# Two-block layer stack on one core: odd stage in another order, first tail weights split ahead of the norms, small products of the even stage in pairs

## The chip, the core and the metric

One core of a Trainium2 chip runs the whole program. Its engines run side by side and meet only at semaphores: TensorE (PE, matrix products into eight PSUM banks), VectorE (DVE), ScalarE (ACT), GpSimd (POOL), and SyncE (SP), which issues nearly all loads. The metric is the device time in microseconds (us) of one execution.

## The reference

Tokens x (256 x 1024) pass a first block of two layers (windowed attention with experts, a bidirectional recurrence with experts; each expert layer reads 16 experts' gate, up and down matrices), and then a second block of two layers, "even" and "odd". All is float32. The change touches the second block and the hand-over to it:

```python
def modulate(x, shift, scale): return layer_norm_2(x) * (1 + scale) + shift
# even: gated linear attention (4 heads, 64 x 128 states, chunks of 64 tokens, both directions d)
att = where(tri, (q*exp(b-b_mid)) @ (k*exp(b_mid-b)).T, 0);  o = att @ v
ds  = (k*exp(b_end-b)).T @ v;   s[c+1] = exp(b_end)*s[c] + ds[c];   o += (q*exp(b)) @ s[c]
y_gla = rms_norm(o) * silu(gg)
# even: latent attention (8 heads of 64+32, 512 keys): y_mla = softmax(q k.T * scale) @ v * silu(mg)
y = concat(y_gla, y_mla) @ w_out;   x = layer_norm_2(ALPHA*x + gate*y, g, b)
# odd: f, f_gate, u, v, s_gate = split(h @ w_in)
y_f = real(fft2(f)) * silu(f_gate)                      # as products with cosine and sine tables
y_s = gelu(u) * (sgu_w @ layer_norm(gelu(v)) + sgu_b) * silu(s_gate)
x = layer_norm_2(ALPHA*x + gate * (concat(y_f, y_s) @ w_out), g, b)
```

## The kernel before

The token axis is two halves of 128 rows, the 1024 features are 8 tiles of 128. The program is written out engine by engine: every engine has its own instruction stream in a fixed order, and `Signals` turns named events into semaphore waits. So a wait at the head of an engine's stream holds everything behind it.

**Weights.** SP loads 2 MB units into a ring of seven slots in a fixed order (`loads`, `units`); a unit's load is issued when the former unit of its slot is "free". A tail unit is split into a rounded part (ACT, L348, four pieces) and the remainder (DVE, L364, four pieces), and each product with it is three passes of TensorE in the rounded format (L324 to L326). Other products are plain float32; the trace shows each of these as two instructions, here called passes.

**Norm and modulation.** After the last expert, DVE adds, takes moments, and norms x half by half (L451, L455, with the root on POOL, L461). `modulated_vector` then takes moments of both halves again (L1726), the root on POOL (L1767), writes `flat` (L1735); TensorE turns `flat` (L1717) between two runs of idle products with the identity (L369); DVE and ACT scale and shift (L1741, L1755), ACT rounds (L1760), DVE takes the remainder (L1746). Only then are the first weights of the stage split (`even_narrow`, `odd_f`).

**Even stage.** After the projections two generators are merged step by step, one step of `linear_*` and one of `latent_*` in turn, on every engine (`even_order`). The linear one: masked scores (L1963, 64 rows of the array a product), turning `kend` (L1973), att times values (L1986), then eight steps, each a read of a direction's state (L1996, 64 output columns of the array) and its state product (L2007), DVE updating the state (L2097), then copies out, squares (L1146), a norm (L1156, L2113), turning (L2022) and `yT` (L2121). States are kept as blocks of a 128 x 256 tile with zeros around them (memsets L2062 to L2064). The latent one: heads' queries and keys (L2220, L2223, one head a step, always output rows 0 to 63), values (L2229), and then 16 score rounds n (L2238, maximum L2324, exp L2378, scaling L2320, turning L2245, copy L2386), with the values product of a head in every second round (L2259, 64 output rows). PSUM banks 4 to 6 take scores and turned scores in turn. When both generators have ended come the output products: half 0 tile by tile (L412, two column blocks), then half 1 column block by column block (L425). `gated_residual_vector` works on a half as its blocks come in (L1780, L1782, L439), then norms it.

**Odd stage.** Five projection units in the order f, sv, su, fg, sg, two jobs each; then the turning of `sgu` (L2439), four rounds of the table products (L2449) and (L2456) with a copy `fc` between (L2501, L2552), the gate products (L2464), and the output products (L412, L425).

## Time and profile before

| | us |
|---|---|
| median of 3 runs | 1600.28 (1597.62 to 1602.88) |
| the profiled execution, device time | 1604.02 |
| its span, first to last instruction | 1602.5 |

Stages in the profiled execution, in us from the span's start: experts of both layers and the first block until about 1254.5, then the tail: hand-over and modulation to 1280.64, projections of the even stage to 1348.78, its two attentions to 1440.9, its output products to 1468.6, norm and modulation to 1488.2, projections of the odd stage to 1547.2, its mixing to 1566.7, its output products to 1594.2, last norm and store to the end. Rows of groups give busy time (overlaps within the group counted once), the mean ns of one instruction, and the idle time before them with what ended it.

### The profile page before, as it was taken

Reading aid. Unit: us, or ns where it says so; the run is one execution under the profiler, and the core shown is the slowest. Engines: PE = TensorE matmul, PEld = TensorE weight load, DVE = VectorE, ACT = ScalarE, POOL = GpSimd, SP = SyncE. Lnnn points to the kernel's source line nnn. Section 1 sums busy time; section 2 is a strip of 40 time slices with the busy share of each in tenths; the row PEclk is TensorE's granted clock in tenths of the full one; section 3 lists DMA queues with packets and bytes.
Section 4 is the critical chain, followed back from the end, with each engine's and each line's share of the span. In section 5 each row is a group of like instructions: output and inputs, shape, how many; then the busy total and the mean of one; then the engine's idle time right before and its main releaser. Section 6 shows DMA issues by size and latency. Waiting matters only on the chain.

```text
span 1602.5 us, 18908 instructions
## 1 busy us (share of the span) xinstructions
PE 1176.6 (73%) x8305; PEld 648.3 (40%) x8305; DVE 460.7 (29%) x940; ACT 299.6 (19%) x594; POOL 62.8 (4%) x88
## 2 busy tenths in 40 slices
PE   7998656687475556988775655656665799989987
PEld 6646211253131113984521111111111597545883
DVE  5535102101111003746420100100100567544524
ACT  4511010000310001291110000000000254340520
POOL 2000100000000000021000000000000100001000
PEclk9998788899778778999897787877867899999999
DMA  9909999999999999445999999999999622107310
GB/s 296 347 0 355 421 425 425 425 416 418 426 426 425 427 426 384 132 152 194 410 424 424 425 427 424 426 427 424 427 425 424 237 86 106 53 14 262 123 53 26
DMA packets 89761, 503.32 MB, mean 314 GB/s; under 512 B 7010, under 2 KB 15664, under 8 KB 56912
## 3 DMA queue, kind: packets, MB, share of 16 engines
q1 hardware_dynamic: 84320, 492.78, 75.9%
q10 hardware_dynamic: 3680, 8.04, 1.4%
q8 instruction: 65, 1.06, 0.3%
q0 software_dynamic: 1680, 1.30, 0.3%
q14 instruction: 16, 0.13, 0.0%
HBM read 501.00 MB, written 1.10 MB: 313 GB/s over the span
## 4 chain that ended last, share of the span: by engine, by line
DMA 50%; PE 33%; DVE 9%; ACT 5%; issue 1%; POOL 1%; SPq 1%; ACTq 0%; DVEq 0%
DMA weight_ring<-in_moe_w_gate_up 29%; DMA weight_ring<-in_moe_w_down 15%; PE bank L1285 5%; PE bank L324 3%; PE bank L325 3%; PE bank L326 3%; PE bank L1312 3%; PE bank L412 3%; DMA weight_spare<-in_ada_w 3%; PE bank L425 3%; DMA weight_ring<-in_even_w_in 2%; DVE weight_ring_rounded L364 1%; PE bank L2259 1%; PE bank L859 1%; DMA weight_ring<-in_lru_w_in 1%
## 5 line engine op out<-in xcount | busy, mean ns | idle before, releaser
L1285 PE MATMUL bank<-weight_ring,expert_tokens 128*32 128x512 f32 x2048 | 321.2, 763 | 205.0 <-DMA weight_ring<-in_moe_w_gate_up 199.0
L1285 PEld LDWEIGHTS bank<-weight_ring,expert_tokens 128*32 128x32 f32 x2048 | 66.6, 125 | 432.2 <-DMA weight_ring<-in_moe_w_gate_up 252.5
L1312 PE MATMUL bank<-weight_ring,actT 128*32 128x256 f32 x2048 | 170.8, 493 | 78.7 <-DMA weight_ring<-in_moe_w_down 68.8
L1312 PEld LDWEIGHTS bank<-weight_ring,actT 128*32 128x32 f32 x2048 | 77.9, 136 | 159.7 <-DMA weight_ring<-in_moe_w_down 68.7
L1406 DVE TENSOR_TENSOR act<-silu,bank 128x256 f32<-128x256 f32 x32 | 13.5, 421 | 435.1 <-ACT silu L1456 435.1
L1411 DVE COPY expert_outs<-bank 32x256 f32<-32x256 f32 x64 | 26.7, 418 | 272.2 <-PE bank L1312 271.2
L1456 ACT ACTIVATE silu<-bank 128x256 f32<-128x256 f32 x32 | 12.3, 384 | 482.0 <-PE bank L1285 481.9
L364 DVE TENSOR_TENSOR weight_ring_rounded<-weight_ring,weight_ring_rounded 128x1024 fp32r<-128x1024 f32 (+1 forms) x64 | 73.4, 1211 | 27.8 <-ACT weight_ring_rounded L348 27.7
L348 ACT CAST weight_ring_rounded<-weight_ring 128x1024 fp32r<-128x1024 f32 (+1 forms) x68 | 65.7, 1044 | 18.2 <-DMA weight_ring<-in_lru_w_in 11.6
L1465 ACT COPY expert_outs<-bank 32x256 f32<-32x256 f32 x64 | 23.3, 365 | 239.4 <-PE bank L1312 238.6
L461 POOL TENSOR_TENSOR norm_rstd<-norm_var,minus_half 128x1 f32<-128x1 f32 x12 | 18.3, 1527 | 932.5 <-DVE norm_var L449 932.5
L1296 PE MATMUL bank<-ident,act 128*128 128x128 f32 x64 | 17.7, 363 | 43.1 <-DVE act L1406 43.1
L1296 PEld LDWEIGHTS bank<-ident,act 128*128 128x128 f32 x64 | 10.1, 206 | 80.5 <-DVE act L1406 80.5
L369 PEld LDWEIGHTS bank<-ident 128*128 128x128 f32 x328 | 38.7, 197 | 1.4 <-issue 1.4
L324 PE MATMUL bank<-lru_x_hi_rounded,weight_ring_rounded 128*128 128x256 f32 x128 | 37.1, 289 | 2.8 <-DVE weight_ring_rounded L1575 1.8
L324 PE MATMUL bank<-odd_h_hi_rounded,weight_ring_rounded 128*128 128x256 f32 x128 | 37.1, 290 | 2.2 <-DVE weight_ring_rounded L364 2.2
L369 PE MATMUL bank<-ident 128*128 128x128 f32 x328 | 38.8, 280 | 0.0
L1329 PE MATMUL bank<-expert_outs,back 128*128 128x512 f32 x64 | 31.7, 622 | 9.3 <-DVE expert_outs L1411 7.9
L325 PE MATMUL bank<-odd_h_rounded,weight_ring_rounded 128*128 128x256 f32 x128 | 36.9, 288 | 0.0
L326 PE MATMUL bank<-odd_h_hi_rounded,weight_ring_rounded 128*128 128x256 f32 x128 | 36.8, 288 | 0.0
L325 PE MATMUL bank<-lru_x_lo_rounded,weight_ring_rounded 128*128 128x256 f32 x128 | 36.6, 286 | 0.0
L326 PE MATMUL bank<-lru_x_hi_rounded,weight_ring_rounded 128*128 128x256 f32 x128 | 36.5, 285 | 0.0
(460 smaller groups left out, 1803.3 us busy)
## 6 DMA issues: line engine op xcount, KB each, us to landing
weight_ring<-in_moe_w_gate_up SPq DMA_DIRECT2D x128, 2048.0 KB, 31.0
weight_ring<-in_moe_w_down SPq DMA_DIRECT2D x64, 2048.0 KB, 31.1
weight_ring<-in_ada_w SPq DMA_DIRECT2D x8, 2048.0 KB, 17.2
weight_ring<-in_even_w_in SPq DMA_DIRECT2D x5, 2048.0 KB, 14.6
weight_ring<-in_odd_w_in SPq DMA_DIRECT2D x5, 2048.0 KB, 8.1
weight_spare<-in_ada_w SPq DMA_DIRECT2D x4, 2048.0 KB, 20.7
weight_ring<-in_lru_w_in SPq DMA_DIRECT2D x4, 2048.0 KB, 23.5
weight_ring<-in_attn_w_qkv SPq DMA_DIRECT2D x2, 2048.0 KB, 15.5
```

Source lines behind the costliest of these rows:

```text
L324: self.pe.matmul(out, sl, mh, start=start, stop=False)
L325: self.pe.matmul(out, sh, ml, start=False, stop=False)
L326: return self.pe.matmul(out, sh, mh, start=False, stop=stop)
L348: a.copy(hi[:, c], raw[:, c]).then_inc(*sig.tell("weights_rounded", ("rounded", name, i)))
L364: v.tensor_tensor(lo[:, c], raw[:, c], hi[:, c], ALU.subtract).then_inc(*sig.tell("weights_split", ("weights", name, i)))
L369: self.pe.matmul(bank[:, 0:P], self.B.ident, self.B.ident, start=True, stop=True)
L412: last = pe.matmul(banks[2 * half + c], y[:, j, rows], w[c][:, j], start=(j == 0), stop=(j == T - 1))
L425: last = pe.matmul(banks[2 + c], y[:, j, P:2 * P], w[c][:, j], start=(j == 0), stop=(j == T - 1))
L1285: last = pe.matmul(up[CAP * j:CAP * (j + 1), :], B.xs[:, t, e * CAP:(e + 1) * CAP], w[:, t % 2, :, j, :], start=(t == 0), stop=(t == T - 1))
L1296: last = pe.transpose(K[2][:, s * P:(s + 1) * P], B.act[i][:, s::2], B.ident)
L1312: last = pe.matmul(K[3][CAP * q:CAP * (q + 1), 0:QC], B.actT[i][:, s, j * CAP:(j + 1) * CAP], w[:, jj, s, q, :], start=(j == 0 and s == 0) ...
L1329: pe.matmul(K[(4, 0)[c]], B.back[:, grp, half * P:(half + 1) * P], B.outs[grp % 2][:, c * 512:(c + 1) * 512], start=True, stop=True).then_ ...
```

## The change

In `experts_pool`, `modulated_vector`, `even_scalar` and `odd_scalar`: ACT rounds the stage's first two units before anything else of the stage, then works out `flat` of half 0 (new `flat_scalar`, six small and large activations with a root on POOL in between); DVE keeps half 1. POOL (new `split_weights_pool`) takes pieces 2 and 3 of `even_narrow`, DVE pieces 0 and 1, between `flat` and the modulation. In the odd stage DVE splits all of `odd_f` inside `gated_residual_vector` of the even stage, after half 0.

Even stage: products that use half of the array's rows or columns are issued in turn for the two halves: masked scores of both k, queries and keys of heads 2j and 2j+1 (the second to rows 64 to 127), values of two heads in every fourth round (with four `pT_lat` buffers). States are compact 128 x 128, without zeros. State products are 64 x 64 blocks of 128 columns over both directions; those of steps 0 and 1 come together, reads (split by row half kk) follow one or two at a time. Squares of `gla` are two activations and one DVE reduction, its scaling one instruction. The output products of tiles 0 to 3 (both halves) are eight more steps of the linear generator, and tiles 4 to 7 follow for half 0 and half 1.

Odd stage: projections f, sv, su; then the first table products and the turning of `sgu`; then fg; then the second table products and the gate products; then sg; then the output products. Banks and DVE's and ACT's orders follow.

```diff
+    def split_weights_pool(self, name, n, pieces):
...
+        for i in pieces:
+            c = slice(i * n // 4, (i + 1) * n // 4)
+            g.wait_ge(*sig.after("rounded", name, i))
+            g.tensor_tensor(lo[:, c], raw[:, c], hi[:, c], ALU.subtract).then_inc(*sig.tell("weights_split_here", ("weights", name, i)))
...
+        stage = f"moe{layer}"
+        self.norm_pool(stage, 0)
+        if layer == 0:
+            self.norm_pool(stage, 1)
+            return
+        narrow = T * sum(n for _, n in EVEN_W[0][1])
+        self.split_weights_pool("even_narrow", narrow, (2,))
+        self.norm_pool(stage, 1)
+        self.flat_pool("even", 0)
+        self.split_weights_pool("even_narrow", narrow, (3,))
+        self.flat_pool("even", 1)
...
     def modulated_tensor(self, stage, banks):
         sig, pe, B = self.sig, self.pe, self.B
+        for c in range(2):
+            pe.wait_ge(*sig.after("summed", BEFORE[stage], 1, c))
         for half in range(H):
...
+    def modulated_vector(self, stage, banks, slot, hi, lo, ahead=lambda: None):
         sig, v, B = self.sig, self.v, self.B
...
+        v.wait_ge(*sig.after("x", BEFORE[stage], 1))
+        for c in range(2):
+            v.bn_stats(B.flat_stats[:, 6 * c:6 * c + 6], B.x[:, 1, c * 512:(c + 1) * 512]).then_inc(*sig.tell("flat_moments"))
+        v.wait_ge(*sig.now("flat_moments"))
+        v.bn_aggr(B.flat_mv, B.flat_stats).then_inc(*sig.tell("flat_moments", ("flat_mean", stage)))
+        v.wait_ge(*sig.after("flat_mean", stage))
+        v.tensor_scalar(B.flat_var[:, 1:2], B.flat_mv[:, 1:2], EPS_SECOND, None, ALU.add).then_inc(
+            *sig.tell("flat_variance", ("flat_variance", stage, 1)))
+        v.wait_ge(*sig.after("flat_deviation", stage, 1))
+        v.tensor_scalar(B.flat[:, 1, :], B.x[:, 1, :], B.flat_mv[:, 0:1], B.flat_rstd[:, 1:2], ALU.subtract, ALU.mult).then_inc(
+            *sig.tell("flat", ("flat", stage, 1)))
+        ahead()
...
+    def flat_scalar(self, stage):
+        sig, a, B = self.sig, self.a, self.B
+        x, flat, mean, square = B.x[:, 0, :], B.flat[:, 0, :], B.flat_sum[:, 0:1], B.flat_sum[:, 1:2]
+        a.wait_ge(*sig.after("x", BEFORE[stage], 0))
+        a.activation(flat, x, ACT.Identity, accum_out=mean).then_inc(*sig.tell("flat_steps"))
...
+        a.activation(flat, x, ACT.Square, bias=mean, accum_out=square).then_inc(*sig.tell("flat_steps"))
...
+        a.wait_ge(*sig.after("flat_deviation", stage, 0))
...
+        a.activation(flat, x, ACT.Identity, scale=B.flat_rstd[:, 0:1], bias=mean).then_inc(*sig.tell("flat_steps", ("flat", stage, 0)))
...
+            if half == 0:
+                between()
...
-        self.out_product_tensor("even", [K[i] for i in self.EVEN_OUT], B.yT, lambda j: ("gla_y", j) if j < GH else ("mla_y", j - GH),
-                                ("even_out0", "even_out1"), (("o_gla", 0), ("o_gla", 1), ("gla_y", 1), ("gla_y", 3)))
+        for half in range(H):
+            self.out_part_tensor(*self.even_out(), half, range(GH, T))
...
+        self.gated_residual_vector("even", [K[i] for i in self.EVEN_OUT], B.even_gate, B.even_tmp,
+                                   lambda: self.split_weights_vector("odd_f"))
...
+        self.split_weights_scalar("even_narrow", T * sum(n for _, n in EVEN_W[0][1]))
+        self.split_weights_scalar("even_qk")
+        self.flat_scalar("even")
...
+        def products(step):
             for i in range(2):
+                for kk in range(2):
+                    for dd in range(2):
+                        c = chunk(dd, step)
+                        rows, at = slice(64 * (c % 2), 64 * (c % 2) + 64), c // 2 * S + i * P + 64 * kk
+                        last = pe.matmul(K[c % 2][64 * kk:64 * kk + 64, step % 2 * S + i * P:step % 2 * S + (i + 1) * P],
+                                         B.kend[dd].rearrange("p a b -> p (a b)")[rows, at:at + 64],
+                                         B.vals[rows, c // 2, (2 * i + kk) * GV:(2 * i + kk + 1) * GV], start=True, stop=True)
+                        if (i, kk) == (1, 1):
+                            last.then_inc(*sig.tell("mixed", ("state_product", dd, step)))
+        def reads(step, kk):
+            for dd in range(2):
+                pe.wait_ge(*(sig.after("state", dd, step) if step else sig.after("states")))
+            r = slice(64 * kk, 64 * kk + 64)
             for i in range(2):
...
+                for dd in range(2):
+                    c = chunk(dd, step)
+                    o = (c // 2 * 2 + i) * GV
+                    last = pe.matmul(out[kk][64 * (c % 2):64 * (c % 2) + 64, o:o + GV],
+                                     B.qb[dd][r, i, c * GCH:(c + 1) * GCH], self.state(dd, step)[r, i, :], start=False,
+                                     stop=(step == NCH - 1), skip_group_check=True)
+                    if i == 1:
+                        last.then_inc(*sig.tell("mixed", ("state_read", dd, step, kk), ("state_read", dd, step)))
+        pe.wait_ge(*sig.after("att", 1, 1))
+        pe.wait_ge(*sig.after("kendT", 1))
+        products(0)
+        products(1)
+        yield
+        reads(0, 0)
+        yield
+        reads(0, 1)
+        reads(1, 1)
+        for dd in range(2):
+            pe.wait_ge(*sig.after("state", dd, 2))
+        products(2)
+        yield
+        reads(1, 0)
+        reads(2, 0)
+        yield
+        reads(2, 1)
+        reads(3, 1)
+        yield
+        reads(3, 0)
...
+            for j in range(GH):
+                self.out_part_tensor(*self.even_out(), half, (j,))
+                yield
...
+        for step in range(NCH - 1):
+            for dd in range(2):
+                c = step if dd == 0 else NCH - 1 - step
+                cur, nxt = self.state(dd, step), self.state(dd, step + 1)
...
+                for i in range(2):
+                    v.scalar_tensor_tensor(nxt[:, i, :], cur[:, i, :], B.end[:, dd, i * NCH + c:i * NCH + c + 1],
+                                           K[c % 2][:, step % 2 * S + i * P:step % 2 * S + (i + 1) * P], ALU.mult, ALU.add).then_inc(
                         *sig.tell("states_moved", ("state", dd, step + 1)))
...
+        for j in range(MH // 2):
...
+                        for i in range(2):
+                            last = pe.matmul(bank[64 * i:64 * i + 64, 0:S], wq[:, k, 2 * j + i, 0:MN], B.cqT[:, k, :],
+                                             start=(k == 0), stop=(k == KQ - 1))
                 else:
                     pe.wait_ge(*sig.after("latT"))
...
+                    for i in range(2):
+                        last = pe.matmul(bank[64 * i:64 * i + 64, :], wkv[:, 2 * j + i, 0:MN], B.latT, start=True, stop=True)
...
+            if n >= 6 and n % 4 == 2:
+                j = n // 4 - 1
...
                 for kt in range(KT):
...
+                    for i in range(2):
+                        last = pe.matmul(bank[64 * i:64 * i + 64, :], B.vals_lat[:, kt, (2 * j + i) * MV:(2 * j + i + 1) * MV],
+                                         B.pT_lat[(2 * j + i) % 4][:, kt, :], start=(kt == 0), stop=(kt == KT - 1))
+                last.then_inc(*sig.tell("values_summed", ("values_lat", j)))
...
+        projection("f")
+        projection("sv")
+        projection("su")
         pe.wait_ge(*sig.after("odd_tables"))
+        for g in range(NG):
+            pe.wait_ge(*sig.after(*(("modulated", "odd", g) if g in (2, 3) else ("odd_taken", g))))
+            for half in range(H):
+                last = pe.matmul(K[self.FC_BANKS[g]][:, half * 2 * P:(half + 1) * 2 * P], B.fT[:, g, half * P:(half + 1) * P], B.dft_c,
+                                 start=True, stop=True)
+            last.then_inc(*sig.tell("mixed", ("fc_product", g)))
...
+        projection("fg")
+        pe.wait_ge(*sig.after("odd_taken", 3))
+        for g in range(NG):
+            pe.wait_ge(*sig.after("fc", g))
...
+        projection("sg")
...
+    ODD_BANKS = (4, 5, 6, 7, 0, 1, 0, 1, 4, 5)
+    ODD_AFTER = (("ident",), ("ident",), ("ident",), ("ident",), ("modulated", "odd", 0), ("modulated", "odd", 1),
+                 ("odd_taken", 4), ("odd_taken", 5), ("fc", 0), ("fc", 1))
+    FC_BANKS = (4, 5, 2, 3)
+    ODD_OUT = (0, 1, 3, 6)
...
-        self.split_weights_vector("odd_f")
...
+        self.split_weights_scalar("odd_f")
+        self.split_weights_scalar("odd_sv")
+        self.flat_scalar("odd")
```

## Rows read from the trace of the kernel before

**Rows 1.** page: the chain that ended last, share of the span by engine

```profile
DMA 50%; PE 33%; DVE 9%; ACT 5%; issue 1%; POOL 1%; SPq 1%; ACTq 0%; DVEq 0%
```

**Rows 2.** stretches: length, busy PE, PEld, DVE, ACT, POOL, granted clock, DMA share, GB/s

```profile
1254.50:1280.64 26.14, 22.13 (x153) 19.21 (x153) 21.41 (x37) 6.38 (x12) 4.49 (x4) 0.93 0.57 200
...
1348.78:1380.90 32.12, 32.12 (x146) 18.16 (x145) 15.71 (x44) 11.22 (x18) 0.00 (x0) 1.00 0.02 4
1380.90:1440.90 60.00, 52.04 (x210) 26.41 (x209) 34.33 (x102) 23.88 (x65) 1.64 (x1) 0.97 0.12 43
1440.90:1468.60 27.70, 27.70 (x66) 12.39 (x67) 9.41 (x15) 0.00 (x0) 1.53 (x1) 1.00 0.63 222
1468.60:1488.20 19.60, 15.21 (x121) 14.83 (x119) 15.18 (x27) 6.36 (x11) 2.97 (x3) 0.91 0.73 256
1488.20:1547.20 59.00, 58.84 (x434) 56.75 (x435) 22.35 (x20) 23.89 (x28) 0.00 (x0) 0.97 0.31 107
1547.20:1566.70 19.50, 13.68 (x70) 11.07 (x69) 9.28 (x35) 1.77 (x3) 1.65 (x1) 1.00 0.00 1
1566.70:1594.20 27.50, 27.46 (x64) 11.80 (x63) 12.63 (x24) 0.00 (x0) 1.52 (x1) 1.00 0.05 19
1410.70:1414.00 3.30, 3.30 (x8) 1.37 (x7) 2.21 (x10) 1.19 (x3) 0.24 (x1) 0.50 0.02 5
```

**Rows 3.** groups of PE, whole span: count, busy us, mean ns, idle before

```profile
L2259 PE MATMUL bank<-mla_pT,mla_values 128*64 128x256 f32 x64 | 17.2, 415 | 0.7 <-ACT mla_pT L2386 0.7
...
L655 PE MATMUL bank<-kT,qT 64*128 64x256 f32 x64 | 9.1, 402 | 2.0 <-ACT at_sink L817 2.0
...
L2220 PE MATMUL bank<-cqT,weight_ring 128*64 128x256 f32 x32 | 8.6, 392 | 0.0
L1996 PE MATMUL bank<-state,qb 128*64 128x256 f32 x32 | 8.6, 390 | 0.0
L2223 PE MATMUL bank<-latT,weight_ring 128*64 128x512 f32 x16 | 8.2, 592 | 0.0
...
L2007 PE MATMUL bank<-gla_values,kend 64*128 64x256 f32 x24 | 6.8, 402 | 0.0
...
L1963 PE MATMUL bank<-qe,ke 64*128 64x128 f32 x32 | 4.6, 285 | 0.0
...
L683 PE MATMUL bank<-pT,qkv 128*64 128x256 f32 x32 | 4.3, 392 | 0.0
```

**Rows 4.** groups of DVE, 1348.7 to 1441, same columns

```profile
L2097 DVE SCALAR_TENSOR_TENSOR state<-state,decay_end,bank 64x128 f32<-64x128 f32 x24 | 8.3, 346 | 0.9 <-PE bank L1996 0.3
```

**Rows 5.** timeline of PE in one score round: start, us, idle before

```profile
1409.96 0.63 PE L2245 MATMUL bank<-ident,mla_scores 128*128 128x128 f32 x4 [2.24 <-DVE mla_scores L2320]
```

**Rows 6.** groups of POOL, whole span

```profile
L461 POOL TENSOR_TENSOR norm_rstd<-norm_var,minus_half 128x1 f32<-128x1 f32 x12 | 18.3, 1527 | 932.5 <-DVE norm_var L449 932.5
L1701 POOL TENSOR_TENSOR i<-i,convolved 128x256 f32<-128x256 f32 x16 | 11.2, 732 | 60.9 <-ACT i L1658 60.7
...
L1767 POOL TENSOR_TENSOR flat_rstd<-flat_var,minus_half 128x1 f32<-128x1 f32 x4 | 2.9, 735 | 9.0 <-DVE flat_var L1731 9.0
```

**Rows 7.** timeline of DVE at the hand-over to the tail

```profile
1261.01 1.28 DVE L455 SCALAR_TENSOR_TENSOR x_tokens<-x_tokens,norm_rstd,norm_bias 128x1024 f32<-128x1024 f32 x1 [0.53 <-POOL norm_rstd L461]
...
1271.88 1.70 DVE L1735 TENSOR_SCALAR flat<-x_tokens,flat_mv,flat_rstd 128x1024 f32<-128x1024 f32 x2 [0.50 <-POOL flat_rstd L1767]
```

**Rows 8.** DMA issues from 1246.2 to 1246.8: KB, us to landing

```profile
weight_ring<-in_even_w_in SPq DMA_DIRECT2D x1, 2048.0 KB, 14.6
```

**Rows 9.** timeline of DVE between the even and the odd stage

```profile
1461.72 0.69 DVE L1780 TENSOR_TENSOR even_tmp<-bank,gate 128x512 f32<-128x512 f32 x1
...
1468.59 0.69 DVE L1780 TENSOR_TENSOR even_tmp<-bank,gate 128x512 f32<-128x512 f32 x1 [4.72 <-PE bank L425]
...
1486.88 9.17 DVE L364 TENSOR_TENSOR weight_ring_rounded<-weight_ring,weight_ring_rounded 128x1024 fp32r<-128x1024 f32 x8
```

**Rows 10.** DMA issues from 1441 to 1452

```profile
weight_ring<-in_odd_w_in SPq DMA_DIRECT2D x2, 2048.0 KB, 10.4
```

More of the change, by code:

```diff
@@ L2012, in linear_tensor, with chunk @@
-        yield
-        for _ in range(3):
+                    o = (2 * half + h // 2) * GV
+                    pe.matmul(out[h % 2][:, o:o + GV], B.att[dd][:, h, half * P:(half + 1) * P],
+                              B.vals[:, half, h * GV:(h + 1) * GV], start=not started[h % 2], stop=False, skip_group_check=True)
+                    started[h % 2] = True
+            if half == 0:
+                yield
+        def chunk(dd, step):
+            return step if dd == 0 else NCH - 1 - step
@@ L2547, in odd_scalar @@
             a.wait_ge(*sig.after("odd", job))
[L2548 removed]
+            a.activation(flat(dst[:, job % 2 * 2:job % 2 * 2 + 2, :]), K[self.ODD_BANKS[job]], ACT.Silu).then_inc(
                 *sig.tell("scalar_moved", ("odd_taken", job)))
[L2550 to L2553 removed]
     def odd_pool(self):
         sig, g, B = self.sig, self.g, self.B
[L2557 removed]
         g.wait_ge(*sig.after("v_variance"))
```

400 lines of the change are left out of this document (170 added, 230 removed).

## The prediction

> **What bounds the kernel now.** I read the page first. Half of the chain that ended last is DMA, a third is PE [rows 1]; the DMA part is the experts' weights, which this change does not touch. It touches only what comes after 1254.5, so next came the stretches of the tail [rows 2]. There PE is busy nearly all the time: 32.12 of 32.12 us and 52.04 of 60.00 in the even stage's two attentions, 27.70 of 27.70 in its output products, 58.84 of 59.00 in the odd projections, 27.46 of 27.50 in the odd output products. DMA moves little there, DVE and ACT are busy about half the time. So in those stretches a microsecond taken from PE is a microsecond of the end. Two stretches are bound by a chain through DVE, POOL and ACT instead: 1254.5 to 1280.64 and 1468.6 to 1488.2, where PE's busy time is mostly idle products; and the odd mixing has 19.50 - 13.68 = 5.8 us without PE work. Then I read the groups of PE by shape [rows 3], which tell what half of the array costs.
>
> **Products in pairs (the largest term).** A pass of 256 columns in half the output columns takes 8.6/32 = 0.27 us when the next pass uses the same half (L2220, L1996; L2259: 17.2/64 = 0.27). Where the first attention gives two halves in turn, it is 9.1/64 = 0.142 (row halves, L655) and 4.3/32 = 0.134 (column halves, L683) [rows 3]. So a pair costs what one did. The groups that are paired now: L2220 8.6, L2223 8.2, L1963 4.6, L1996 8.6, L2007 6.8, L2259 17.2, together 54.0 us. After: 4.3 + 4.1 + 2.3 + 8.6 for the queries, keys, masked scores and values. Reads become 64 passes of 128 columns in quarters of the array, taken as two at a time: half of L683's time each, 64 x 0.067 = 4.3. Products become 24, or 48 passes of 128 columns, in quarters too, taken as four at a time; one pass of 128 columns alone is 4.6/32 = 0.144, so 48 x 0.144/4 = 1.7. Sum 25.3, so PE loses 28.7 us. No row shows a quarter of the array in turn with another: bounds are no overlap at all (64 x 0.144 - 4.3 = 4.9 and 48 x 0.144 - 1.7 = 5.2 more, together 10) and this sum. I take the sum, since rows and columns each overlap in full.
>
> From 1348.78 to 1468.6 (119.8 us) PE works 32.12 + 52.04 + 27.70 = 111.9 and idles 8.0 [rows 2]. After, it works 83.2. Idle after: with less to do, PE meets waits that were covered. State updates: eight DVE instructions of 0.346 us [rows 4], now 128 rows high, must be done before the products of step 2 (2.0 us open, since only short reads lie between), then 0.65 and 0.4 at later steps. One norm of `gla` through ACT, DVE and POOL must end before its turning in round 8: 1.7. The first `gla_y` after it 0.9, the last copy of turned scores 0.7, and 3.0 us for the rest of the score rounds. These are 8.7 (range 4 to 16). The score rounds before show idle pieces ahead of a turning that waits for DVE, the longest 2.24 us, when ACT was at the eight squares of `gla` (now two instructions) [rows 5]; the eight output steps (27.7/16 = 1.7 us each) lie in rounds 10 to 17 and cover those there. Result: 83.2 + 8.7 = 91.9 us, **27.9 us saved** (range 20 to 31).
>
> **Front of the even stage.** Before, ACT casts the first weights only after the modulation and DVE takes `flat` of both halves, ending at 1273.58 (1271.88 + 1.70 [rows 7]). After, ACT's casts lie at 1255.6 to 1259.4 and, since `even_qk` is issued at 1246.3 and takes 14.6 us [rows 8], from 1261 to 1264.9; they hold the stream that the later `flat` of half 0 is in, which then ends near 1270. It is not late: half 1 comes last. DVE without half 0 would end `flat` of half 1 at 1271.6; POOL's piece 3 in front of the root adds 1.1, giving 1272.7. A POOL piece of 896 columns has no row; by 0.70 to 0.73 us for 256 [rows 6] it is 2.5 us. The two weight pieces that DVE takes ahead of the modulation (2.1 us) lie under the turning and the 16 idle products. PE then starts near 1277.7 (1272.7 and 5.0 for turning, first modulation and idle products) instead of 1280.64: 3.0, and 0.8 of stalls on the weights goes too. Against it: POOL's piece 2 starts at about 1261.0, exactly with DVE's L455 [rows 7]. The root of one column takes 1.53 us in L461, beside DVE's L451, and 0.73 in L1767, beside nothing of that kind [rows 6]; so one engine can hold the other up. If POOL holds DVE through its piece, the chain is 2.4 later and the part saves 1.4, or 0.5 if piece 3 holds DVE too; if it goes the other way, it saves all 3.8. I take **2.2 us** (range 0.5 to 4.5).
>
> The Trainium skill, "SBUF — State Buffer", Who interferes with whom, says that a VectorE instruction with two SBUF inputs contends with a GpSimd one that reads SBUF, and that the first to issue keeps the other out entirely. The trace agrees by 1.53 against 0.73 us; by the rule alone this part is worth whichever of 0.5 and 3.8 us the order at 1261.0 gives.
>
> **Between the stages.** Call E' the end of the even output products. Before, column block 0 of half 1 was ready early (DVE at 1461.72) and only block 1 was left at 1468.59 [rows 9]. Now half 1's two blocks both end at E'. Half 0 ends on DVE at E' + 0.7, and only then does DVE split `odd_f`: half of the 9.17 us that eight such pieces took [rows 9], 4.6. Its data is there: the load takes 10.4 us from its issue near 1450 of the old time [rows 10], and the cast by ACT is behind it. Half 1 then begins at E' + 5.3. Before, one block and the norm took 6.0 from E; the second block adds three instructions of 0.69, so half 1 is normed at E' + 13.3. Moments, root and `flat` of half 1 add 3.3 us, so E' + 16.6. Before, 8.5 us lay between `flat` and PE's first weight product at E + 19.6; of these the first split piece, 1.2, goes, and 1.0 for the modulation that waited behind `flat` of both halves: E' + 22.9. Before, there were 3.3 us more of stalls on splits and of half clock (0.91 in the mean [rows 2]) after the start; the first job ended at E + 27.4 and would now end at E' + 28.7. So 1.3 us is lost. Here the 4.6 us of splitting comes onto the path and the split that stood ahead of PE goes; the edit trades one for the other. If PE finds its start earlier, up to 3 us come back.
>
> **Odd stage.** `fg` now runs between the first table products and the second, and covers the copies of `fc` that PE waited for; `sg` covers the rest. The 5.8 us without PE work go [rows 2]. PE's work stays, so after the start: 56.6 of projections (58.84 less some 2 of lower clock at a mean of 0.97), 13.7 and 27.5 = 97.8 [rows 2]. E' to the end of the output products is 22.9 + 97.8 = 120.7 against 1594.2 - 1468.6 = 125.6: **4.8 saved** (range 1 to 8), the net of both parts. The other loads stay ahead of their use by several microseconds.
>
> **Sum.** 1604.0 (profiled execution) - 2.2 - 27.9 - 4.8 = 1569.1. That execution stands 3.7 us above the median of the runs, so the median after is about 1565.4; I say 1566.
>
> **Rivals.**
> A, the forecast: 0.60, 1559 to 1573.
> B, the score chain sets the pace. Turning of round n-2 waits for the exponential, sum and scaling of round n-2, with DVE and ACT also serving the copies; PE's cover by values products is halved (8.6 us go), and they come in every fourth round. For: such an idle piece stands there already [rows 5]. Against: ACT and DVE are busy under 60% there [rows 2]. If each of 16 rounds waits 0.45 us more, that is 7: 1573. Chance 0.15.
> C, quarters of the array do not overlap (no row shows them). Of the 10 us more, some 2 fall into the wait for the states, so 8: 1574. Chance 0.10.
> D, all covers hold: DVE is not held by POOL, waits are short: 4.5 instead of 2.2, 5 us less idle: 1558. Chance 0.08.
> E, pairs do not overlap although they do in L655 and L683, since the weights here are loaded between every two passes: the change doesn't do what it says. 28.7 less saved, of which PE's waits would hide 2.5: 1592. Chance 0.04.
> F, slower than before. With sparser work PE drops to its lower clock. In 1410.7 to 1414.0 the granted clock is 0.50, that is 1.2 of 2.4 GHz, and PE is busy on without a gap [rows 2], right after 2.24 us in which it was idle [rows 5]. Gaps of 2.0 us open now at the state chain and between rounds. PE's work at full clock is 83 us in the two attentions and the output products; each microsecond of it at the lower clock costs one more. It is slower than before if more than 35 us of it run so; with 50 it is 1615. Against: pieces of work between gaps are longer than the gaps everywhere. Chance 0.03.
>
> The Trainium skill, "TensorE: Matmul & The Clock Gate", HAM oscillation — how this bites in real kernels, tells of a kernel whose every burst starts at the lower clock because a wait stands before each; it would make this F. The trace here shows one such stretch in 60 us.
>
> **Range and chances.** C and B lie at the upper end, D at the lower; 1556 to 1578 holds A to D but their tails, about 0.8. Faster by over 0.3% (4.8 us, about what a measurement of this kernel can tell from no change) holds for A to E: 0.95; within 0.3%: 0.02; slower: F, 0.03.
>
> **What would show it.** Groups of L2220, L2223, L2259 and reads at half their busy time with the same mean each; state products near 1.7 us; the stretch from the end of the projections to the end of the even output products near 92 us with 9 idle. Half 1's `flat` near 1272.7 and PE's start near 1277.7; POOL's piece near 2.5 us, with L455 beside it long or not. DVE's four pieces of `odd_f` right after half 0, half 1 from E' + 5. No idle time ahead of L2456's successor. Wrong would be: a granted clock under 0.9 in the attentions, idle time of over 16 us there, or pairs that take twice the time.

## Result and profile after

The changed kernel took 1573.92 us (median of 4, 1567.92 to 1577.5) against 1600.77 before: a ratio of 0.983 (95% interval 0.981 to 0.985), 26.9 us less. Run again beside the experiments it took 1566.85 us, a ratio of 0.980 (0.978 to 0.982) to before on the same chip. The forecast was 1566 with a range of 1556 to 1578; both results lie in the range, the first 8 us above the forecast and the second 1 us above it. The traced execution of the first result was its fastest, 1567.92 us. Its page and its stretches (length; busy PE, PEld, DVE, ACT, POOL; granted clock, DMA share, GB/s), to be held against [rows 2]:

```profile
span 1566.6 us, 18985 instructions
```

```profile
1277.22:1344.52 67.30, 65.73 (x489) 61.74 (x487) 43.93 (x85) 32.17 (x52) 1.41 (x2) 1.00 0.32 114
1344.52:1369.40 24.88, 23.09 (x192) 13.84 (x196) 15.28 (x46) 12.89 (x22) 0.00 (x0) 1.00 0.24 85
1369.40:1372.80 3.40, 3.40 (x22) 1.91 (x22) 0.79 (x2) 0.00 (x0) 0.00 (x0) 0.51 0.00 0
1372.80:1389.90 17.10, 12.66 (x88) 6.89 (x86) 11.72 (x31) 9.05 (x21) 1.64 (x1) 1.00 0.00 1
1389.90:1393.30 3.40, 3.25 (x10) 2.33 (x11) 0.66 (x3) 0.00 (x0) 0.00 (x0) 0.51 0.00 0
1393.30:1439.80 46.50, 44.95 (x169) 22.14 (x168) 21.50 (x52) 15.10 (x30) 1.53 (x1) 1.00 0.28 102
1439.80:1461.05 21.25, 15.05 (x122) 14.70 (x120) 17.91 (x28) 12.12 (x20) 2.63 (x3) 0.84 0.93 326
1461.05:1558.30 97.25, 97.25 (x567) 78.39 (x565) 40.33 (x75) 20.46 (x25) 4.08 (x2) 1.00 0.20 71
```

The middle (end of the even projections to last even output product) is 95.3 us long, 119.7 before, and its clock falls to 0.51 twice, for 3.4 us each. From 1461.05 to 1558.30 PE has no idle time at all. By stage, in us, from events that both kernels have:

| stretch | before | after, first trace | after, second trace | forecast |
|---|---|---|---|---|
| until the first residual add behind the experts | 1256.1 | 1255.4 | 1250.2 | as before |
| to the first even weight product | 24.5 | 21.9 | 23.7 | 21.6 |
| even projections | 68.2 | 67.3 | 67.4 | 67.4 |
| middle | 119.7 | 95.3 | 101.3 | 91.9 |
| hand-over to the first odd weight product | 19.6 | 21.2 | 21.8 | 22.9 |
| odd stage to its last output product | 106.0 | 97.3 | 97.3 | 97.8 |
| rest | 8.3 | 8.3 | 8.3 | 8.3 |

The products in pairs, by groups of PE in the middle (count; busy us, mean ns), against [rows 3]:

```profile
L2346 PE MATMUL bank<-mla_pT,mla_values 128*64 128x256 f32 x64 | 7.8, 385 | 0.7 <-ACT mla_pT L2472 0.7
L2306 PE MATMUL bank<-cqT,weight_ring 128*64 128x256 f32 x32 | 4.3, 392 | 0.0
L2311 PE MATMUL bank<-latT,weight_ring 128*64 128x512 f32 x16 | 4.1, 592 | 0.0
...
L2072 PE MATMUL bank<-state,qb 64*64 64x128 f32 x48 | 3.5, 277 | 0.0
L2016 PE MATMUL bank<-qe,ke 64*128 64x128 f32 x32 | 2.3, 284 | 0.3 <-DVE att L2162 0.3
L2057 PE MATMUL bank<-gla_values,kend 64*64 64x128 f32 x48 | 2.1, 315 | 1.2 <-DVE state L2181 1.2
```

Same mean, half the busy time; the state products in quarters took 2.1 us (1.7 forecast; 1.8 in a kernel below where the clock was full), the reads 3.5 + 1.3 = 4.8 (4.3).

### The profile page after: what moved, and what is told of

The parts are those of the page before. It is cut to its first block, busy times and chain, and to the rows that moved or that the text cites. A ratio compares the mean times of both kernels' runs of the same rounds, so it can differ in the third digit from the quotient of the medians.

```text
span 1566.6 us, 18985 instructions
## 1 busy us (share of the span) xinstructions
PE 1140.2 (73%) x8361; PEld 635.7 (41%) x8361; DVE 447.2 (29%) x902; ACT 306.7 (20%) x596; POOL 67.9 (4%) x90
## 4 chain that ended last, share of the span: by engine, by line
issue 29%; PE 28%; DMA 26%; DVE 9%; ACT 4%; POOL 1%; SPq 1%; DVEq 0%; ACTq 0%; POOLq 0%
DMA weight_ring<-in_moe_w_gate_up 11%; DMA weight_ring<-in_moe_w_down 10%; PE bank L423 3%; PE bank L324 3%; PE bank L325 3%; PE bank L326 3%; PE bank L1296 3%; DMA weight_spare<-in_ada_w 3%; DMA weight_ring<-in_even_w_in 2%; PE bank L436 2%; PE bank L1323 2%; DVE weight_ring_rounded L364 1%; PE bank L870 1%; PE bank L2326 1%; POOL norm_rstd L472 1%
## 5 line engine op out<-in xcount | busy, mean ns | idle before, releaser
L1323 PE MATMUL bank<-weight_ring,actT 128*32 128x256 f32 x2048 | 167.6, 485 | 80.7 <-DMA weight_ring<-in_moe_w_down 71.4
L1307 PE MATMUL bank<-ident,act 128*128 128x128 f32 x64 | 17.3, 356 | 43.0 <-DVE act L1417 43.0
## 6 DMA issues: line engine op xcount, KB each, us to landing
weight_ring<-in_ada_w SPq DMA_DIRECT2D x8, 2048.0 KB, 17.3
weight_ring<-in_even_w_in SPq DMA_DIRECT2D x5, 2048.0 KB, 14.7
```

Of the source, the lines that this page charges most:

```text
L1323: last = pe.matmul(K[3][CAP * q:CAP * (q + 1), 0:QC], B.actT[i][:, s, j * CAP:(j + 1) * CAP], w[:, jj, s, q, :], start=(j == 0 and s == 0) ...
```

## Experiments

Each ratio is to the kernel before on the same chip. "The stretch" is the middle of the table. Idle products, or fills, are products with the identity whose results nobody reads.

**The changed kernel again.** No edit.

> The changed kernel once more, for a second trace and more times: its runs spread over 9.6 us (1567.9 to 1577.5) and the traced one was the fastest. Theory 1, the clock: TensorE falls to half clock after idle time in the even stage's attentions, in some executions more often than in others. Then a trace of a slower execution has a lower granted clock between 1344 and 1440 and again between 1440 and 1461, and the stages before the tail agree within 1 us. Theory 2, the experts: the difference lies before the tail, where the loads set the pace. Then the tail (from the first weight product of the even stage to the end, 289.4 us in the traced execution) agrees within 1 us and what is before differs. Median expected near 1573.

Measured: 1566.85 us, 6 us under the 1573 that was expected. Both theories hold for a part. Before the tail this trace is 5.1 us shorter (loads set the pace there), and the tail is 8.4 us longer, 6.0 of it in the stretch. Its stretches there:

```profile
1341.29:1366.40 25.11, 23.31 (x201) 14.07 (x204) 15.51 (x46) 12.89 (x22) 0.00 (x0) 1.00 0.23 84
1366.40:1383.20 16.80, 16.80 (x80) 9.97 (x71) 6.35 (x20) 3.77 (x10) 0.00 (x0) 0.50 0.01 1
1383.20:1391.20 8.00, 5.28 (x28) 2.23 (x27) 5.60 (x13) 5.01 (x12) 1.64 (x1) 0.93 0.00 0
1391.20:1397.00 5.80, 5.16 (x15) 3.52 (x16) 2.52 (x7) 0.81 (x2) 0.00 (x0) 0.50 0.00 0
```

For 16.8 us PE is busy without a gap at half clock, right after the wait for the states. At full clock that work would be 8.4 us. Busy time of the stretch is 94.4 us; less half of the 22.0 us at half clock it is 83.4, the forecast's 83.2. Of the other traces without fills there, four show this long form (split later, no weights on GpSimd, `flat` first, old odd order: 101.2 to 101.5 us, 17 to 20.5 us at half clock from this wait on). The first trace shows the short one, 3.4 us. In the trace with the loops swapped the same wait of 1.2 us brings no fall at all. What decides between the three is not shown.

**Fills in every wait.** 32 idle products between half 0 and 1 of the odd turning, 54 instead of 36 ahead of it, and:

```diff
         reads(1, 1)
+        pe.wait_ge(*sig.after("latent_taken", MH + 3))
+        self.idle_products_tensor(K[7][:, S:2 * S], 9)
...
+        self.idle_products_tensor(K[7][:, S:2 * S], 12)
         pe.wait_ge(*sig.after("o_normed"))
...
+                if n == 7:
+                    pe.wait_ge(*sig.after("mla_y", 0))
+                    self.idle_products_tensor(K[7][:, S:2 * S], 10)
                 pe.wait_ge(*sig.after("probs_lat", i))
```

> Idle products are put where PE waits: 9 before the state products of step 2, 10 before the turning in score round 7, 12 before the turning of gla, 32 between the two halves' turning in the odd stage and 18 more ahead of it. Theory 1, the clock: two stretches of 3.2 us each at half clock between 1344 and 1440 cost 3.3 us and one after 1455 some 1 us; all of it goes, PE's busy time of real work there falls from 87.3 to 84, and the median falls by 3 to 6 us, more if the slower executions are slower for that reason. Theory 2, the chain through DVE, ACT and POOL sets the pace in those places: the clock is 1.00 but the stretch is as long as before within 1 us, since PE then only waits longer.

Measured: 1569.26 us, ratio 0.981 (0.978 to 0.983), no better than the changed kernel. The stretch took 94.4 us at clock 1.00, the hand-over 24.3:

```profile
1340.85:1435.23 94.38, 90.75 (x536) 52.39 (x537) 49.96 (x131) 37.09 (x74) 3.17 (x2) 1.00 0.20 73
1435.23:1459.54 24.31, 24.31 (x220) 24.31 (x220) 16.92 (x26) 11.77 (x20) 2.63 (x3) 1.00 0.82 287
```

The clock theory holds for the cause, not for the sum. The fills were sized too long: 32 idle products ran 7.31 us where `flat` was ready after 2.5, so the hand-over lost 4.6.

**The split of `odd_f` later.**

```diff
-        self.gated_residual_vector("even", ..., B.even_tmp, lambda: self.split_weights_vector("odd_f"))
+        self.gated_residual_vector("even", ..., B.even_tmp)
...
-        self.modulated_vector("odd", K, 2, B.h_hi["odd"], B.h_raw["odd"])
+        self.modulated_vector("odd", K, 2, B.h_hi["odd"], B.h_raw["odd"],
+                              lambda: self.split_weights_vector("odd_f", pieces=(0, 1)))
+        self.split_weights_vector("odd_f", pieces=(2, 3))
```

> DVE's split of odd_f is taken out from between the two halves of the even stage's residual; two pieces go behind flat of half 1, two behind the modulation. Theory 1, the split lies on the path: half 1's residual starts 4.5 us earlier and flat ends 4.5 us earlier; the two pieces ahead of the modulation cost about 0.5 and PE's first weight product comes 3 to 4.5 us earlier after the end of the even output products (21.2 us in the changed kernel). Rival: the cast and turning, or the pieces that are split late, hold PE instead: the first product comes earlier but the first job waits for pieces 2 and 3, and the gain is under 1 us.

Measured: 1572.48 us, ratio 0.983 (0.981 to 0.985). The hand-over took 20.7 us, 0.6 to 1.1 less than in the two traces of the changed kernel. DVE's half 1 did start 4.5 us earlier, and stood before its second scaling:

```profile
1454.09 1.28 DVE L466 SCALAR_TENSOR_TENSOR x_tokens<-x_tokens,norm_rstd,norm_bias 128x1024 f32<-128x1024 f32 x1 [3.30 <-POOL norm_rstd L472]
```

```profile
1452.90 0.56 POOL L1804 TENSOR_TENSOR flat_rstd<-flat_var,minus_half 128x1 f32<-128x1 f32 x1 [9.23 <-ACT flat_var L1780]
1453.43 0.55 POOL L472 TENSOR_TENSOR norm_rstd<-norm_var,minus_half 128x1 f32<-128x1 f32 x1
```

GpSimd's root of half 1's norm stands behind that of half 0's `flat`, which waits for ACT, and ACT was at the cast of `odd_sv` from its landing at 1446.1. The gain was lost to an order that had been hidden under the split.

**Loops swapped.**

```diff
-                    for k in range(KQ):
-                        for i in range(2):
+                    for i in range(2):
+                        for k in range(KQ):
...
-                for kt in range(KT):
-                    for i in range(2):
+                for i in range(2):
+                    for kt in range(KT):
```

> Same products, banks and events as the changed kernel, but the heads' queries and the values products are issued one head after the other instead of in turn (the two loops swapped). Theory 1, only passes in different halves that follow each other overlap: values products take 17 us instead of 7.8, queries 8.6 instead of 4.3; together 13 more for PE, of which waits hide some, so 10 to 13 us slower. Rival: the chain through DVE and ACT sets the pace of the score rounds, so PE has room: under 5 us slower.

Measured: 1578.49 us, ratio 0.985 (0.983 to 0.988). In the trace the queries cost what they did (4.4 us) and the values 11.4, not 17; the stretch took 97.4 us. Eight passes of one head and then eight of the other take 2.86 us, in turn 1.95:

```profile
1382.08 2.86 PE L2346 MATMUL bank<-mla_pT,mla_values 128*64 128x256 f32 x16
```

So the expectation's premise was wrong: four passes in one half followed by four in the other overlap in full, eight by eight in part. The experiment does not take the overlap away. The time moved more than the trace explains: the median is 11.6 us above the changed kernel's on the same chip, with intervals apart, while the traced execution, the fastest, has a stretch 2.1 us longer than the first trace's (3.6 more in the values products, 1.7 less by the fall that is missing). The slower executions may have had the long form of half clock, some 6 us more; they left no trace, so this stays open.

**No weights on GpSimd.** The two calls of `split_weights_pool` go, and DVE splits pieces 2 and 3 ahead of `even_qk`.

> GpSimd splits no weights; DVE splits pieces 2 and 3 of even_narrow behind the modulation instead. Theory 1, the collision costs what the prediction feared: DVE's second scaling of half 0 falls from 3.05 back to 1.28 us and the root of half 1 no longer waits behind a piece, so flat of half 1 ends 2 to 2.8 us earlier (17.3 us after the first residual add in the changed kernel, 14.5 to 15.3 here); 1.2 to 1.5 of it is given back as stalls of the first job on pieces 2 and 3, so its end comes about 1 earlier. Rival: the pieces cost as much behind the modulation as they cost on GpSimd, and the end of the first job is not earlier or is later.

Measured: 1565.5 us, ratio 0.979 (0.976 to 0.981). DVE's second scaling is back to 1.28 us:

```profile
1255.94 1.28 DVE L466 SCALAR_TENSOR_TENSOR x_tokens<-x_tokens,norm_rstd,norm_bias 128x1024 f32<-128x1024 f32 x1 [0.53 <-POOL norm_rstd L472]
```

`flat` of half 1 ends 15.5 us after the first add (17.3 and 17.9 in the changed kernel), but PE, idle from 1265.0 to 1266.9 because ACT's `flat` of half 0 waited for the cast of `even_qk`, turned and filled at half clock, and the first product came at 22.8 us after the first add. No stall of the first job followed (projections 67.3). Against the second trace (23.7) that is 0.9 earlier, against the first (21.9) 0.9 later, and the ratio's interval holds the changed kernel's 0.980: a gain is not shown.

**`flat` first on ACT.** The split later as above, and in both stages

```diff
-        self.split_weights_scalar("even_qk")
         self.flat_scalar("even")
+        self.split_weights_scalar("even_qk")
...
-        self.split_weights_scalar("odd_sv")
         self.flat_scalar("odd")
+        self.split_weights_scalar("odd_sv")
```

> Two orders changed against the changed kernel: DVE's split of odd_f is out of the residual as in the run before (0.5 to 1.1 us there, since ACT was at the cast of odd_sv when half 0 was ready, and the root of half 1's norm on GpSimd stood behind half 0's), and ACT works out flat of half 0 before it casts the second unit, in both stages. Theory: the chain from the landing of the second unit through that cast to GpSimd's roots was what took the split's place. Then DVE's 3.3 us of idle before half 1's second scaling goes, flat of half 1 ends near 11 us after the end of the even output products (15.3 in the changed kernel), PE's first product comes near 17.5 (21.2 to 21.8), and the even stage starts 21.9 after the first add in every execution. Rival: the first odd job waits for pieces 2 and 3 or odd_sv's later cast is late for its job, and 2 or 3 us come back as stalls in the odd stage (97.3 us from first to last product).

Measured: 1565.95 us, ratio 0.979 (0.977 to 0.981). Even start at 21.85, hand-over 16.9 instead of 21.2 to 21.8: DVE's wait went as said, so the split and the cast's order together held 4.3 to 4.9 us. The odd stage took 97.7. The stretch had the long form of half clock:

```profile
1337.82:1439.19 101.37, 94.96 (x474) 51.48 (x475) 50.17 (x131) 37.01 (x73) 3.16 (x2) 0.88 0.19 68
```

**All of it, fills fitted.** The former, with 5 idle products before the wait for the states, 6 before the turning of score round 7 and 7 before that of `gla`; 26 (instead of 36) and 17 in the hand-over, 6 between the even halves.

> The former with idle products of fitted number: 5, 6 and 7 at the three waits of the attentions (9, 10 and 12 had kept the clock at 1.00 but came to about 2.5 us more than the waits), 26 and 17 in the hand-over to the odd stage (54 and 32 had held PE for 4.6 us after flat was ready), 6 between the halves of the even stage. Theory 1, the clock: the stretch from the projections' end to the last even output product takes 92 to 94 us in place of 95.3 and 101.3, the hand-over 16.5; device time 1560 to 1564. Rival: the shorter fills leave gaps after which the clock falls anyway, and the stretch takes 95 to 101 as before.

Measured: 1556.81 us (1554.05 to 1559.9), ratio 0.973 (0.971 to 0.975). It beats both kernels, and its interval lies clear of both of the changed kernel's.

```profile
1337.59:1429.71 92.12, 88.28 (x510) 49.55 (x511) 49.92 (x131) 37.00 (x73) 3.16 (x2) 1.00 0.21 75
1429.71:1445.31 15.60, 15.24 (x136) 14.89 (x134) 14.11 (x24) 11.66 (x20) 2.85 (x3) 1.00 0.99 367
1445.31:1544.41 99.10, 97.76 (x564) 78.50 (x564) 43.94 (x79) 21.00 (x27) 4.07 (x2) 1.00 0.23 82
```

```profile
L369 PE MATMUL bank<-ident 128*128 128x128 f32 x38 | 5.0, 278 | 0.0
```

Less 5.0 us of idle products PE works 83.3 us in the stretch and has 8.8 without work. Forecast were 83.2 and 8.7. The rival of stalls holds for a small part: the first odd job waits 1.35 us for pieces 2 and 3 (1.19 at 1448.15, 0.16 at 1449.29).

**The odd stage in the old order.** `odd_tensor`, `odd_vector`, `odd_scalar` and the banks of before; casts, `flat` and DVE's split where the change put them.

> The odd stage's order, banks and engine orders of the kernel before in the changed kernel (casts and flat of half 0 stay where the change put them, and DVE's split of odd_f too). Theory: fg and sg between the table products cover all of the copies, so without them 5.8 us of waits come back: 103 us from the first to the last product of the odd stage instead of 97.3. Rival: the odd stage gained because its first job no longer stalls on splits and half clock (3 us of the 106.0 before), so 1 to 3 us come back only, or the whole 8.7.

Measured: 1579.24 us, ratio 0.987 (0.985 to 0.989). The odd stage took 105.8 us, so all 8.6 come back and the rival is right about the size, not about the reason, since its projections run without idle time (57.21 of 57.21 us). In the mixing (20.97 long):

```profile
1519.98:1540.95 20.97, 15.15 (x69) 12.03 (x68) 9.10 (x35) 1.77 (x3) 1.65 (x1) 0.92 0.00 0
```

```profile
1528.47 3.33 PE L2542 MATMUL bank<-dft_n,fc 128*128 128x256 f32 x8 [3.60 <-DVE fc L2586]
```

20.97 - 15.15 = 5.8 us are without PE work, as forecast. Eight passes after the longest wait take 3.33 us where the next eight take 2.00 (the clock is 0.92 in the mean); the kernel before had this wait too, at a clock of 1.00 [rows 2], so these 1.3 us belong to this trace. The remaining 1.4 was not taken apart.

**No weights on GpSimd, with fills.** The kernel with fitted fills and the edit of "No weights on GpSimd"; between the even halves stand 2 idle products instead of 6.

> The kernel with fitted fills and the two orders changed, and no weight pieces on GpSimd; 2 idle products instead of 6 between the halves of the even stage. Theory: without the collision and without the root behind a piece, flat of half 1 ends 15.0 to 15.5 us after the first residual add (17.3 with GpSimd's pieces) and the first product comes at 20.3 to 20.8 instead of 21.85; no stall on pieces 2 and 3, as the run without GpSimd's pieces showed none (projections 67.3 us). 1 to 1.5 us faster than the kernel with all fills, about 1555. Rival: the first job, now earlier against the splits, waits for pieces 2 and 3 and the projections take 68.5: no gain.

Measured: 1557.24 us, ratio 0.973 (0.970 to 0.975), the same as with GpSimd, and its stretch is 92.1 us at full clock too. The first product comes 1.8 us earlier (20.1) and the first job then waits for a piece; the projections take 68.9:

```profile
1274.40 0.30 PE L324 MATMUL bank<-even_h_hi_rounded,weight_ring_rounded 128*32 128x256 f32 x1 [1.13 <-DVE weight_ring_rounded L364]
```

**One fill only.** The changed kernel with the 5 idle products before the wait for the states.

> The changed kernel with one fill only: 5 idle products while PE waits for the states before the products of step 2. Theory: this wait, 1.2 us after a row of small products, is what the clock falls on: half clock from 1366.6 to 1383 in most traces, 3.2 us in the first one. With the fill the clock is 1.00 until the wait for gla's norm near 20 us later, falls there for 3 to 5 us as before, and the stretch takes 93.5 to 95 us instead of 95.3 or 101.3 to 101.5; times near 1565. Rival: the waits that follow it take its place and the clock falls a few us later for as long.

Measured: 1565.38 us, ratio 0.978 (0.975 to 0.980).

```profile
1346.54:1389.20 42.66, 38.76 (x307) 23.03 (x306) 26.65 (x76) 21.00 (x41) 1.63 (x1) 1.00 0.15 50
1389.20:1396.30 7.10, 5.78 (x16) 3.70 (x17) 3.18 (x7) 2.11 (x6) 0.01 (x1) 0.52 0.00 0
1346.54:1441.31 94.77, 87.86 (x485) 48.20 (x485) 50.03 (x131) 37.05 (x73) 3.16 (x2) 0.96 0.21 73
```

Full clock until the wait for the norm, then 7.1 us at half. None of the six traces with a fill before the wait for the states has a fall there, six of the seven without one have: the long form hangs on this wait. In device time the one fill is not resolved, since its interval overlaps the changed kernel's.

**Output products late.** The fitted kernel without the eight output steps among the score rounds; all tiles at the end.

> The kernel with fitted fills and orders, but the output products of tiles 0 to 3 come at the end with the others instead of one in each of eight score rounds. Theory, cover: a score round of PE alone is 1.46 us, its chain through DVE and ACT longer (idle pieces of 0.5 to 0.9 us before each turning), so 0.5 to 1 us a round of new idle, 4 to 8 us in all, and the clock may fall on top: the stretch from the projections' end to the last even output product 96 to 104 instead of 92.1. Rival: DVE and ACT keep up with 1.5 us a round and it stays under 94.

Measured: 1561.87 us, ratio 0.975 (0.973 to 0.978). The stretch took 96.4 us at full clock, 4.2 more than with them: the lower end of what was expected. PE's idle time accounts for 2.6 of it (6.5 against 3.8 us), nearly all before turnings that wait for DVE's scaling (4.1 against 1.5). The other 1.6 is PE's busy time with the same products and was not taken apart.

**Both heads in the same half.** The second head's queries, keys and values onto the first's output rows, and head after head as in "Loops swapped"; the first head's numbers are lost.

```diff
-                            last = pe.matmul(bank[64 * i:64 * i + 64, 0:S], wq[...
+                            last = pe.matmul(bank[0:64, 0:S], wq[...
```

> Same products in the kernel with fitted fills and orders, but the second head of each pair writes queries, keys and values into the same 64 output columns of the array as the first (so its results overwrite the first's, and what follows works on wrong numbers). This takes the overlap of two halves away and nothing else. Theory: a pass of 256 columns takes 0.27 us instead of 0.13: values 16.5 to 17.2 instead of 7.8, queries 8.6 instead of 4.3, keys 8.2 instead of 4.1, 17 us more of PE, of which waits of 2 to 4 us hide some: the stretch takes 105 to 109 instead of 92.1. Rival: the array's halves matter little where weights are loaded between passes: under 98.

Measured: 1570.83 us, ratio 0.981 (0.979 to 0.984).

```profile
L2353 PE MATMUL bank<-mla_pT,mla_values 128*64 128x256 f32 x64 | 14.7, 382 | 0.7 <-ACT mla_pT L2479 0.7
...
L2310 PE MATMUL bank<-cqT,weight_ring 128*64 128x256 f32 x32 | 7.8, 385 | 0.0
L2315 PE MATMUL bank<-latT,weight_ring 128*64 128x512 f32 x16 | 7.5, 592 | 0.0
```

30.0 us for what takes 16.2 in two halves; the stretch 105.1 against 92.1. Of 13.8 us more work 13.0 arrive at the end. Two things change at once here; for the values products "Loops swapped" has the order alone, 11.4 us, so of the 6.9 us from 7.8 to 14.7 the order takes 3.6 and the shared half 3.3.

## Why the forecast came out as it did

**Products in pairs** (28.7 of PE's work): right in mechanism and size. Halves were halves, quarters overlapped too (C falls: 2.1 + 4.8 us, not 10 more), E falls by the same groups, and the same-half kernel shows that 13 of 14 us of such work reach the end. The row of values products before, 17.2 [rows 3], had one of its eight groups at half clock, 3.58 us where the others took 1.94: at full clock it is 15.6. The same 1.6 us stand in the 111.9 of PE's work before, so they cancel in the 83.2, which is work at full clock.

**The middle** (91.9): right at full clock, 92.1 with the fitted fills, wrong as the kernel stands, 95.3 and 101.3, the second of them outside its range of 20 to 31 us saved. The failed step is the one under F, "pieces of work between gaps are longer than the gaps everywhere": I took it for a reason that the clock stays up, and priced the clock only as a rare case of the whole stretch. It falls in all seven traces without fills: PE works 3.4 us at half clock with the loops swapped, 6.7 in the first trace, 22.5 in the second and 23.1 to 23.9 in the other four. Half of that is lost, and some of the loss hides waits: against the 92.1 with fitted fills the middle is 3.2 and 9.2 us longer in the two traces of the changed kernel. F's mechanism was right, its chance and its size were not: not 35 us or nothing, but some of it always. The row that showed it, 3.3 us at 0.50 after 2.24 us of idle [rows 2, 5], stood in the forecast as a rival and belonged in the sum. The Trainium skill's account of the clock ("TensorE: Matmul & The Clock Gate", HAM oscillation — how this bites in real kernels) fits what both traces show, a wait and then a burst at the lower clock. It tells of short bursts between long waits; that half clock stays for 16.8 us of work without a gap, after a wait of 1.2 us, is what the second trace adds.

The idle time was summed wrongly. The terms listed for it (2.0, 0.65, 0.4, 1.7, 0.9, 0.7 and 3.0 us) add up to 9.35, not 8.7, so the middle should have read 92.6 and the sum 1569.8. In the first trace PE is idle for 7.9 us: 1.2 for the states where 2.0 was forecast, 1.7 for the norm of `gla` as forecast, 0.4 for the first `gla_y`, 0.7 for the last copy of turned scores, 3.4 in the other score rounds, and 0.6 for masked scores that no term had.

**B**, the score chain as the pace, is not what happened: with fills the time without real work was 8.8 us, near the forecast. The place of the eight output steps is worth 4.2 us, of which 2.6 are waits that they cover (output products late).

**Front** (2.2 saved, range 0.5 to 4.5): 3.6 in the first trace (2.6 and 0.9 of stalls), 1.7 in the second (0.8 and 0.8). The collision came, as feared, at the very instruction:

```profile
1260.24 3.05 DVE L466 SCALAR_TENSOR_TENSOR x_tokens<-x_tokens,norm_rstd,norm_bias 128x1024 f32<-128x1024 f32 x1 [0.53 <-POOL norm_rstd L472]
```

```profile
1260.12 2.09 POOL L380 TENSOR_TENSOR weight_ring_rounded<-weight_ring,weight_ring_rounded 128x896 fp32r<-128x896 f32 x1
...
1268.46 2.86 POOL L380 TENSOR_TENSOR weight_ring_rounded<-weight_ring,weight_ring_rounded 128x896 fp32r<-128x896 f32 x1
```

3.05 us instead of 1.28 with GpSimd's piece 0.12 us ahead: 1.77 lost, not 2.4, and piece 3, beside DVE's scaling of half 1, was the late one there (2.86 against 2.09). By the Trainium skill's rule ("SBUF — State Buffer", Who interferes with whom) the first to issue keeps the other out. Both rows agree: GpSimd was first at 1260.12, DVE was first at 1268.07. What was missed: ACT's cast of `even_qk` waits for its landing. It began 4.9 us after the first add in the first trace and 7.1 in the second, where it held `flat` of half 0 and, through GpSimd's root and piece 3, half 1's root. `flat` of half 1 came only 0.6 us later by that. The other 1.2 of the 1.8 us are the clock: PE waited 2.30 us for `flat` of half 0, and half 1's turning with the 16 idle products took 5.8 us at a mean granted clock of 0.75, where the first trace has 4.5 at 1.00:

```profile
1266.44 1.13 PE L1739 MATMUL bank<-ident,flat 128*128 128x128 f32 x8 [2.30 <-ACT flat L1785]
1268.15 1.97 PE L1739 MATMUL bank<-ident,flat 128*128 128x128 f32 x8 [0.58 <-DVE flat L1754]
```

The trace with one fill, whose experts end as late as the first trace's (1255.2) and whose cast begins 6.4 us after the add, has the same delay (23.96), so it is the landing against the add that decides and not how early the experts end.

**Between the stages** (E' + 22.9, first job's end E' + 28.7): 21.2 to 21.8, and with 48 passes of 0.12 and no stall the job ends near 27. Order and cause were right (`between` on the path; without it and with `flat` first 4.3 to 4.9 us less), the term was 1.1 to 1.7 too large. Its "3.3 us more of stalls and of half clock" after the old start disagrees with its own E + 27.4: 19.6 and 48 passes of 0.12 leave 2.0. The sum does not use it. Two waits of PE lie in the hand-over, 2.17 and 4.02 us with 1.14 us of turning between, and the clock is at 0.50 from 1451.4 to 1458.2:

```profile
1450.01 1.14 PE L1739 MATMUL bank<-ident,flat 128*128 128x128 f32 x8 [2.17 <-ACT flat L1785]
1455.17 1.97 PE L1739 MATMUL bank<-ident,flat 128*128 128x128 f32 x8 [4.02 <-DVE flat L1754]
1456.93 4.36 PE L369 MATMUL bank<-ident 128*128 128x128 f32 x32
```

**Odd stage**: 97.3 against 97.8 forecast, no idle time; the order alone is worth 8.6 in the one trace of it, of which the 5.8 of waits were counted and 1.3 are half clock.

**Sum**: in the first traced execution the terms give 1569.1 and the trace 1567.9, by an error of +3.4 in the middle against -1.4 in front, -2.3 behind and -0.8 before the tail. The agreement is luck by 3 us. Why the other executions of the first result took 1573.5 to 1577.5 stays open, since they left no trace. Their mean granted clock was 0.863 to 0.872 against 0.883 in the traced one, which would fit more half clock; but one execution of the second result took 1566.3 us at 0.864, so the mean does not decide. The second trace shows that the middle can be 6 us longer and the part before the tail 5 us shorter.

## What to carry to other kernels

When work is taken from an engine whose clock depends on being busy, sum at both clocks: look for every wait that opens between short pieces, and count work behind it at the lower clock. A few idle products fitted to such a wait (here 18 in three places, each row within 0.3 us of its wait) took the stretch from 101.4 to 92.1 us in the traces; too many cost what they bought. And before an edit is moved off a path, look at what else is queued on the small engines: here one order gave 0.6 to 1.1 us by itself, and 4.3 to 4.9 once a second order was changed.

## What the runs showed that I had not expected

- Half clock can outlast its cause: 16.8 us of PE work without a gap at 0.50 after a wait of 1.2 us (1364.9 to 1366.1), in another execution of the same instructions 3.4 us. Five idle products ahead of that wait kept the clock at 1.00 there in all six traces that had them or more.
- Products in different halves of the array need not alternate: 4 passes and then 4 take as long as in turn (1.09 us), 8 and then 8 take 2.86, in turn 1.95, all 16 in one half 3.67.
- Fills are worth what they fit to: 54 and 32 idle products gave a hand-over of 24.3 us at full clock, longer than the 21.2 and 21.8 with 36 and none; 26 and 17, with the two orders changed, 15.6 against 16.9 with 36 and none.
